# Attention stage: row tile 1 prepared first, output weights' upper halves on ScalarE, first key pages loaded in the stage, head squares in small pieces

## The reference, cut to what matters

```python
xn = _rms(x, norm_g)
q, k, v, g_c, qi, wi, ki, xq, g_x = _split(xn @ w_in, ODD_SPLITS)   # 8 query heads, 2 key heads of 128
q = _rope(_rms(heads(q, AT_HEADS), qn), pos)
k = _rope(_rms(heads(k, AT_KV_HEADS), kn), pos)
...                                       # indexer: scores of qi and ki, the 256 best keys of each query are kept
s = einsum('bqngd,bqknd->bqngk', qg, kg) * Dh ** -0.5
p = softmax(where(valid, s, -inf));  yC = einsum(p, vg) * silu(g_c)
yX = _mem_attn(heads(xq, XA_HEADS), mk, mv, mem_qn) * silu(g_x)
y = concatenate([yC, yX]) @ w_out;  x + y         # w_out_odd: 1536 rows x 1024 columns
```

## Time and profile before

| | |
|---|---|
| median of 3 runs | 1815.67 us |
| the profiled execution | 1824.58 us, its span 1823.0 us |
| TensorE busy | 1726.9 us (95%), 9077 matmuls |
| weight loads of TensorE | 1327.7 us (73%) |
| VectorE busy | 954.1 us (52%) |
| ScalarE busy | 592.3 us (32%) |
| GpSimd busy | 423.5 us (23%) |
| granted TensorE clock, mean | 0.978 |

### The profile page before, as it was taken

How to read it: one execution, slowest core, us unless ns; L and a number is a source line. 1 busy time by engine, 2 the same in 40 slices (tenths; PEclk the granted TensorE clock), 3 DMA queues, 4 the chain that set the end, 5 groups by cost and what they waited for, 6 DMA issues and landing times. The chain is left out here.

```text
span 1823.0 us, 25878 instructions
## 1 busy us (share of the span) xinstructions
PE 1726.9 (95%) x9077; PEld 1327.7 (73%) x9077; DVE 954.1 (52%) x2238; ACT 592.3 (32%) x1256; POOL 423.5 (23%) x665
## 2 busy tenths in 40 slices
PE   6999999999999998998999999999889689998999
PEld 5666788777788787886875567787667467776887
DVE  5512643224677564213540668888868664685111
ACT  3110332111122113102211447788745444552010
POOL 4301221100243451000352002211016553510000
PEclk9999999999999999999999999999999789998999
DMA  6333342554575567212233122334442754334231
GB/s 222 127 115 116 120 120 99 168 169 139 175 207 169 160 207 277 104 68 90 69 97 95 52 66 89 104 100 151 151 151 70 261 177 134 117 113 133 97 121 47
DMA packets 145196, 239.18 MB, mean 131 GB/s; under 512 B 21222, under 2 KB 75398, under 8 KB 145066
## 3 DMA queue, kind: packets, MB, share of 16 engines
q1 hardware_dynamic: 120650, 172.75, 29.3%
q0 software_dynamic: 18352, 57.29, 10.0%
q10 hardware_dynamic: 6064, 7.47, 1.2%
HBM read 171.21 MB, written 66.17 MB: 130 GB/s over the span
## 5 line engine op out<-in xcount | busy, mean ns | idle before, releaser
L1285 PE MATMUL ring_acc<-ring_w_hi,layer_xT_hi 128*128 128x512 f32 x640 | 261.0, 408 | 0.2 <-PE all_banks L1428 0.2
L1287 PE MATMUL ring_acc<-ring_w_hi,layer_xT_lo 128*128 128x512 f32 x640 | 249.9, 390 | 0.0
L1286 PE MATMUL ring_acc<-ring_w_lo,layer_xT_hi 128*128 128x512 f32 x640 | 249.6, 390 | 0.0
L2869 PE MATMUL front_acc<-front_w_hi,front_xT_hi 128*128 128x512 f32 x520 | 219.8, 423 | 17.3 <-DVE front_w_lo L3349 5.5
L2870 PE MATMUL front_acc<-front_w_lo,front_xT_hi 128*128 128x512 f32 x520 | 206.2, 397 | 0.0
L2871 PE MATMUL front_acc<-front_w_hi,front_xT_lo 128*128 128x512 f32 x520 | 206.2, 397 | 0.0
L1285 PEld LDWEIGHTS ring_acc<-ring_w_hi,layer_xT_hi 128*128 128x128 f32 x640 | 120.3, 188 | 32.0 <-issue 9.1
L2869 PEld LDWEIGHTS front_acc<-front_w_hi,front_xT_hi 128*128 128x128 f32 x520 | 99.3, 191 | 57.5 <-issue 18.8
L1287 PEld LDWEIGHTS ring_acc<-ring_w_hi,layer_xT_lo 128*128 128x128 f32 x640 | 120.1, 188 | 26.3
L1286 PEld LDWEIGHTS ring_acc<-ring_w_lo,layer_xT_hi 128*128 128x128 f32 x640 | 120.4, 188 | 25.3 <-issue 2.6
L3183 ACT ACTIVATE front_index_rows<-odd_bias,front_candidate,front_minus_sign 128x1024 bf16<-128x1024 f32 (+1 forms) x124 | 132.5, 1073 | 10.9 <-DVE front_candidate L3498 10.8
(11 more groups left out here) (712 smaller groups left out, 3495.9 us busy)
## 6 DMA issues: line engine op xcount, KB each, us to landing
all_w<-in_w_even POOLq DMA_DIRECT2D x80, 256.0 KB, 3.7
h_even<-layer_st SPq DMA_DIRECT2D x79, 256.0 KB, 2.2
all_w<-in_w_odd POOLq DMA_DIRECT2D x61, 256.0 KB, 3.5
h_odd<-front_st SPq DMA_DIRECT2D x55, 256.0 KB, 2.1
layer_scratch<-h_even SPq DMA_DIRECT2D x46, 256.0 KB, 3.1
all_scratch<-in_w_mem SPq DMA_DIRECT2D x32, 256.0 KB, 3.6
all_scratch<-h_even SPq DMA_DIRECT2D x32, 256.0 KB, 3.5
all_scratch<-x SPq DMA_DIRECT2D x14, 512.0 KB, 3.7
```

What stands on the lines that cost most here:

```text
L1285: T.matmul(out[0:rows, :], xh[:, kk, to], wh[:, r, :], start=(kk == 0), stop=False)
L1286: T.matmul(out[0:rows, :], xh[:, kk, to], wl[:, r, :], start=False, stop=False)
L1287: ins = T.matmul(out[0:rows, :], xl[:, kk, to], wh[:, r, :], start=False, stop=(kk == KC - 1))
L2869: T.matmul(out[0:rows, :], xh[:, k, to], wh[:, r, :], start=(k == 0), stop=False, skip_group_check=True)
```

## The change

1. In the front, ScalarE's head stream starts two steps later and is cut into more pieces: key squares in four pieces of 4 heads, query squares in two of 4, scales in pieces of 5, 5 and 6 key heads and of 4 and 4 query heads. To place them it is advanced a second time in each of slots 63 to 71, ahead of the unit's eviction (`amid`); on all other engines `qk_amid` does nothing.
2. SyncE's 16 loads of the first key pages move from slot 69 of the front into the attention stage, behind the loads of the first three row tiles, ahead of the loads of the bias rows.
3. In the attention stage row tile 1 is prepared ahead of the sample's rows.
4. The upper halves of w_out_odd are made by ScalarE, behind the exponential of the slot; VectorE makes the lower halves only. The slots with two slices come first (four of them), then 16 with one.

```diff
@@ front_plan @@
     for s in range(62, 73):
         plan[s].append("qk")
+    for s in range(63, 72):
+        amid[s] = ["qk_amid"]
@@ SyncE, loads_qk @@
-                yield
-                sp.wait_ge(vmix, NB)
-                for _ in range(2):
-                    yield
-                for _ in range(3):
+                for _ in range(6):
                     yield
                 sp.wait_ge(bd, 3)
                 sp.dma_start(c.bias_rows[:, :, :], bc(smp, 1, 8)).then_inc(b_out, 16)
                 yield
-                sp.wait_ge(split_d, UNITS // T1 * KC)
-                for u in range(2):
-                    first_keys(u, [c.raw[KVH * u + n] for n in range(KVH)], n_pool)
                 yield
                 yield
                 sp.wait_ge(krq, 1)
@@ SyncE, end of the front @@
-            sp.wait_ge(kp_in, 16 * 2 * 4 * KVH)
@@ ScalarE, head_squares @@
+                yield
+                yield
                 act.wait_ge(k_rows_in, 32)
-                squared(KR, k_ssq, range(0, 8), ksq)
-                yield
-                act.wait_ge(ksq, 1)
-                squared(KR, k_ssq, range(8, 16), ksq)
-                yield
+                for n in range(4):
+                    if n >= 2:
+                        act.wait_ge(ksq, n - 1)
+                    squared(KR, k_ssq, range(4 * n, 4 * n + 4), ksq, 2048 + 512 * (n % 2))
+                    yield
                 act.wait_ge(q_rows_in[0], 16)
-                act.wait_ge(ksq, 2)
-                squared(c.q_rows[0], c.qk_ssq[0], range(QH), hsq)
-                yield
+                for n in range(2):
+                    act.wait_ge(ksq, n + 3)
+                    squared(c.q_rows[0], c.qk_ssq[0], range(4 * n, 4 * n + 4), hsq, 2048 + 512 * n)
+                    yield
                 act.wait_ge(krs, 1)
-                scaled(KR, k_ssq, range(16)).then_inc(ksc, 1)
-                yield
+                for hs in (range(0, 5), range(5, 10), range(10, 16)):
+                    scaled(KR, k_ssq, hs).then_inc(ksc, 1)
+                    yield
                 act.wait_ge(q_rows_in[1], 16)
-                squared(c.q_rows[1], c.qk_ssq[1], range(6), hsq6, 3072)
-                act.wait_ge(hsq6, 1)
-                squared(c.q_rows[1], c.qk_ssq[1], range(6, QH), hsq, 3072)
+                squared(c.q_rows[1], c.qk_ssq[1], range(4), hsq, 3072)
+                yield
+                act.wait_ge(hsq, 3)
+                squared(c.q_rows[1], c.qk_ssq[1], range(4, QH), hsq, 3072)
                 yield
                 for u in range(2):
                     act.wait_ge(hrs, u + 1)
-                    scaled(c.q_rows[u], c.qk_ssq[u], range(QH)).then_inc(hsc, 1)
-                    yield
+                    for hs in (range(0, 4), range(4, QH)):
+                        scaled(c.q_rows[u], c.qk_ssq[u], hs).then_inc(hsc, 1)
+                        yield
                 yield
                 act.wait_ge(ktu, 1)
                 A(c.kT[:, :, :].rearrange("p h t -> p (h t)"), c.banks[:, :], ACT.Copy).then_inc(c.kT_made, 1)
                 while True:
                     yield
+            heads_of_rows = head_squares()
             follow(plan, UNITS, dense, amid, norm=squares(), prep=copies(), smp=smps(), index=relus(), find=finds(), mem=mems(), cached=exps_of_cached(),
-                   qk=head_squares(), copy=copies_of_mems(), cached_copy=cacheds(), decide=idle())
+                   qk=heads_of_rows, qk_amid=heads_of_rows, copy=copies_of_mems(), cached_copy=cacheds(), decide=idle())
...
@@ layer1_back @@
-    TILE, PREP = [L] + ROW_TILES, [L] + ROW_TILES[2:]
+    TILE, PREP = [L] + ROW_TILES, ROW_TILES[2:3] + [L] + ROW_TILES[3:]
...
-    TURN = [8, 8, 9, 9, 9, 9, 9]
+    TURN = [7, 8, 9, 9, 9, 9, 9]
...
-    TURNED = lambda p: 2 * p + 1
-    SPLITS = [[w] for w in range(16)] + [[w, w + 1] for w in range(16, 2 * OUT_CHUNKS, 2)]
+    TURNED = lambda p: 2 * p + 1 if p else 2
+    SPLITS = [[w, w + 1] for w in range(0, 8, 2)] + [[w] for w in range(8, 2 * OUT_CHUNKS)]
...
@@ SyncE, behind load_rows(2) @@
+                for u in range(2):
+                    for p in range(4):
+                        page = key_page(sp, u, p)
+                        for n in range(KVH):
+                            sp.dma_start(c.raw[KVH * u + n][:, P * p:P * p + P], page[:, n, :]).then_inc(k01_in, 16)
@@ TensorE @@
             def smp_scores(m):
                 if m == 0:
                     pe.wait_ge(sqc, 1)
+                    pe.wait_ge(k01_in, 16 * 2 * 4 * KVH)
@@ ScalarE @@
+            def weights():
+                yield
+                yield
+                act.wait_ge(sst, 16 * 2 * 4)
+                for ws in SPLITS:
+                    for w in ws:
+                        k, half = divmod(w, 2)
+                        act.wait_ge(w_in[w % RAW], 16 * (w // RAW + 1))
+                        A(wh[:, k, 512 * half:512 * half + 512], raw[w % RAW], ACT.Copy).then_inc(whi, 1)
+                    yield
@@ VectorE, weights @@
-                dve.wait_ge(sst, 16 * 2 * 4)
                 for ws in SPLITS:
                     for w in ws:
                         k, half = divmod(w, 2)
                         e = slice(512 * half, 512 * half + 512)
-                        dve.wait_ge(w_in[w % RAW], 16 * (w // RAW + 1))
-                        split(V, link, raw[w % RAW], wh[:, k, e], wl[:, k, e]).then_inc(wsd, 1)
+                        dve.wait_ge(whi, w + 1)
+                        V.tensor_tensor(wl[:, k, e], raw[w % RAW], wh[:, k, e], ALU.subtract).then_inc(wsd, 1)
                     yield
```

79 lines of the change are left out of this document (37 added, 42 removed).

## The result

The changed kernel took 1828.45 us (median of 6 runs, 1822.36 to 1832.54), the kernel before 1816.06 in the runs beside it (6 runs, 1814.96 to 1823.91): a ratio of 1.0061 with a 95% interval of 1.0037 to 1.0085, that is 7 to 15 us slower. The forecast was 1822.8 us, in a range of 1815 to 1833. The profiled execution took 1832.54 us.

A forecast was written before the change was run, and what follows sets the result against it. TensorE was taken as the bound nearly everywhere, so edits count by its gaps. Terms 1.2 - 2.8 + 15.7 - 4.5 - 2.5 = +7.1 gave 1831.7 us for the profiled execution, median 1822.8, range 1815 to 1833.

The forecast's parts named there:

- The gaps of the front: Front: TensorE's 5.48 and 4.50 us gaps mostly go, -13.5 with slow matmuls; VectorE meeting GpSimd's key scaling gives +1.7.
- The key copy one slot late: Front, slot 71: ScalarE's key copy stands behind the bias write, TensorE idles +10.6 us, then lower clock +2.4.
- The front's sum: Front: gaps, key copy wait and lower clock together +1.2 us, bounds -2.8 to +3.6.
- First key pages: Loads moved from front to attention stage: 0, as they held up no TensorE work and land before the first sample scores.
- Start of the stage: Attention stage, row tile 1 first: 3.67 us TensorE gap goes, larger load costs 0.8; -2.8 us, bounds 0 and -3.7.
- the 4.14 us wait of VectorE goes; next is TensorE's own score work: Attention stage's start: VectorE no longer waits for GpSimd's roots of row tile 1; TensorE's score work, ending 1433.6, then limits.
- where nobody waits for them before slot 9: Attention stage: GpSimd's 10 us of work on the sample moves behind tile 1's roots, with nobody waiting before slot 9.
- Weights: Slots 46 to 63, output weights split: ScalarE and VectorE wait for each other, 68.3 us against 52.6, +15.7.
- The end: Near the end: 3.66 us weight transfer wait goes, -4.5; the low clock behind TensorE's 4.47 us gap goes, -2.5.
- The 4.8 us of engine time: Weights: 24 slices rounded in 0.63 us on ScalarE against 0.43 on VectorE; the wait chain costs three times that.
- the difference of 8.9 us between profile and median: Whole kernel: profiled execution before was 8.9 us above the median 1815.67, carried over unchanged to the changed kernel.
- the turn-taking: Weights' slots: rounding waits behind the exponential, subtraction for rounding, next masking behind subtraction; 3.38 us for 512 columns, 3.77 for 640.

The follow-up runs named there:

- front_copy_early: Kernel before with the front's part alone, but ScalarE's copy of the transposed keys one advance earlier: 1818.06 us, ratio 1.0013.
- keys_late: Kernel before with only the 16 first key page loads moved into the attention stage: 1816.31 us, ratio 0.9997.
- rows_first: Kernel before with only row tile 1 prepared ahead of the sample's rows: 1820.81 us, ratio 1.0040.
- before_again: Kernel before with no edit, run once more for a second profile: 1817.54 us (1 run).
- pairs_first: Kernel before with only the slice order changed, four two-slice slots first, both halves on VectorE: 1808.99 us, ratio 0.9967.
- upper_act_ahead: Kernel before with the weights' part alone, ScalarE's rounding of a slice one slot ahead of VectorE's subtraction: 1813.36 us, ratio 0.9987.

## Why the prediction came out as it did

**The gaps of the front (-13.5, +1.7): right.** 0.69 instead of 5.48 us, 1.21 instead of 4.50. VectorE met GpSimd's key scaling as forecast (VectorE, then GpSimd, in the changed kernel):

```profile
1372.94 4.46 DVE L3608 TENSOR_TENSOR front_need<-front_ties,all_over 32x1 f32<-32x1 f32 x1
```

```profile
1372.78 4.61 POOL L2785 TENSOR_TENSOR front_index_rows<-front_index_rows,all_scratch 128x2048 f32<-128x2048 f32 x1 [6.57 <-ACT front_index_rows L3284]
```

The Trainium skill says in "Trainium Architecture — The Big Picture", section What this means for kernel authors, that the port pair of VectorE and GpSimd is locked exclusively and not shared in bandwidth. The trace agrees: the instruction began 0.16 us behind GpSimd's and ended with it, and its own size (one column, 0.14 us in the kernel before) did not matter.

**The key copy one slot late (+10.6, +2.4): right.** 10.40 us. The counted yields decided this, and they were enough: 18 advances put the copy ahead of unit 70's eviction, the 19th behind the wait for the ties. The front's sum, +1.2, measured +0.8 in the changed kernel's profile and about +1.2 over all profiles. front_copy_early shows the price of the advance, 8.5 us in the front instead of 13.0, of which 4.2 come back at the start of the next stage.

**First key pages (0): right,** by keys_late, 0.2 us apart with an interval of -2.2 to +1.3.

**Start of the stage (-2.8, bounds 0 and -3.7): wrong, in size and sign.** Measured are +2.4 to job 14 and +1.0 to job 46; where the clocks agree it is +1.0 to +2.3 and then +3.9 (rows_first against front_copy_early) to +4.2 (changed against before_again), so that the order costs 5 to 6.5 us, which fits the +6.1 of rows_first's median. The step that failed is "the 4.14 us wait of VectorE goes; next is TensorE's own score work": next was VectorE's rotation, which moved ahead of job 5's masking and ran beside GpSimd's work on the sample, the very work that the prediction had called harmless ("where nobody waits for them before slot 9"). Nobody waits for GpSimd's result, but VectorE's instructions beside it took 2.3 us longer. I had weighed this contention in the front and not here. The later meeting near job 27 (3.8 us) comes from the same order, and no bound that I gave held a price above 0.

**Weights (+15.7): right,** +15.0 (over 17 slots; the forecast counts the slot of job 63 as well), with slots of 3.35 and 3.72 us. **The end (-4.5, -2.5): right,** -7.1. pairs_first shows that this belongs to the order of the slices and would come without ScalarE. The 4.8 us of engine time that the prediction named beside it are the small part; the cost was the order of waits: upper_act_ahead has the same 24 instructions on ScalarE and is 11 us better against its base.

**The sum.** +7.1 was forecast for the profiled execution, +11.9 measured in the stretches that the change touches; the start of the stage is 6.2 of the difference, and the others make up -1.4. That the difference of 8.9 us between profile and median would carry over was wrong too: it was 4.1 after. The part ahead of the change varies by itself (1342.8 to 1349.0 us in fourteen profiles), and so does the clock in the stage's first 23 jobs.

That the median, 1828.45 us, came out within the range is in part luck. The two large terms, the late key copy and the turn-taking, were right in mechanism and size. But the order of the rows costs 5 to 6.5 us where a gain of 2.8 was forecast, and no bound of that term reaches it. The time lies in the range thanks to the room left above the other terms.

## What to carry to other kernels

When work is handed from one engine to another within one step of a software pipeline, write down where the handed instruction stands in both streams: behind a dependent of this step it makes the engines take turns, and one step ahead most of that goes (10.2 of the 13.5 us that it cost against pairs_first between jobs 46 and 63). In streams that are advanced by a plan, count the yields: an edit that splits work into more pieces moves everything behind them, and the one that another engine waits for decides. Where GpSimd's large elementwise work is moved, look for every VectorE instruction that will then run beside it, however small and whoever waits for GpSimd. Before a stretch of one profile is laid to an edit, compare its granted clock with that of the other profile.

## What the runs showed of the hardware

- A VectorE instruction on 128x1 or 32x1 numbers (0.14 to 0.22 us) took 2.76, 2.85 and 4.46 us when it met a GpSimd multiplication of 2.36 or 4.61 us, and ended with it. The 4.46 us stand in all seven profiles with the front's part, the 2.76 and 2.85 in the two with row tile 1 first.
- Between two stages the barrier came no sooner than 9.03 us after GpSimd's last instruction, three times within 0.01 us, with the other engines idle at the end.
- The same program's stretch from job 14 to job 46 took 123.7 and 120.5 us in two executions, at mean granted clocks of 0.94 and 0.97. The stretch to job 14, with the same instructions, took 56.7 us in one kernel and 53.2 in another, at 0.77 and 0.82. One profile of each kernel doesn't tell such a difference from the edit's; the clock of the stretch does.
- Costs of parts by medians didn't add up: +9.6, +6.1 and +8.5 alone, +12.4 together, with intervals of 2 to 4 us each. By stretches with like clocks they come to 1.2, 5 to 6.5 and 7.9, that is 14 to 16, against 7 to 15 for the interval of the changed kernel's median.
